# A fused two-block transformer layer on one core: where small side products of TensorE stand

## The reference

```
sh1, sc1, gt1, sh2, sc2, gt2 = split(silu(c) @ w_mod + b_mod, 6)       # w_mod: 1024 x 6144
csh1, csc1, ...              = split(silu(c_ctx) @ w_mod + b_mod, 6)
h  = rmsnorm(x, g_pre1)   * (1 + sc1)  + sh1
hc = rmsnorm(ctx, g_pre1) * (1 + csc1) + csh1      # ctx: 256 context tokens
q, k, v, f, g_a, g_f = split(h @ w_in);  kc, vc = split(hc @ w_in[:, k and v])
attn = banded_window_attention(rope(q), rope(k), v, kc, vc, sink)
y = (sigmoid(g_a) * (attn @ w_pa) + sigmoid(g_f) * (fourier_mix(f) @ w_pf)) @ w_out
x = x + gt1 * rmsnorm(y, g_post1)
h2 = rmsnorm(x, g_pre2) * (1 + sc2) + sh2
x = x + gt2 * rmsnorm(conv_ffn(h2), g_post2)
```

## Time and profile before

| | us |
|---|---|
| median of 3 runs | 1402.28 (1400.53 to 1405.31) |
| profiled execution: its time | 1401.24 |
| profiled execution: span | 1399.5 |
| TensorE busy | 1372.2 (98%) |
| DVE busy | 839.5 (60%) |
| ACT busy | 636.2 (45%) |

### The profile page before, as it was taken

How to read it: one execution, slowest core, us unless ns; L and a number is a source line. 1 busy time by engine, 2 the same in 40 slices (tenths; PEclk the granted TensorE clock), 3 DMA queues, 4 the chain that set the end, 5 groups by cost and what they waited for, 6 DMA issues and landing times.

```text
span 1399.5 us, 17278 instructions
## 1 busy us (share of the span) xinstructions
PE 1372.2 (98%) x6886; PEld 1116.6 (80%) x6886; DVE 839.5 (60%) x1272; ACT 636.2 (45%) x1032; POOL 26.9 (2%) x28
## 2 busy tenths in 40 slices
PE   8999999999999999999999999999999999999998
PEld 6777766788888888888987777887888888888887
DVE  6577887487766767665846444346466543444334
ACT  7435566554545444234534544444544333333234
POOL 3000000000003000000000000000000000000000
PEclk9999999999999999999999999999999999999999
DMA  6524220323222333663031111132214432222321
GB/s 242 203 83 135 76 76 31 121 106 124 102 89 92 98 98 124 237 211 121 31 129 61 47 61 61 60 121 90 91 44 136 142 115 90 94 102 91 105 91 61
DMA packets 46043, 146.71 MB, mean 105 GB/s; under 512 B 4971, under 2 KB 12139, under 8 KB 45580
## 3 DMA queue, kind: packets, MB, share of 16 engines
q1 hardware_dynamic: 45676, 145.08, 31.3%
q10 hardware_dynamic: 288, 0.52, 0.1%
HBM read 142.18 MB, written 3.41 MB: 104 GB/s over the span
## 4 chain that ended last, share of the span: by engine, by line
PE 88%; DVE 6%; ACT 3%; DMA 2%; issue 1%; SPq 0%; DVEq 0%; ACTq 0%
PE PS L351 26%; PE PS L352 25%; PE PS L353 25%; PE PS L1056 1%; PE PS L1047 1%; DVE wlo L317 1%; DVE mt L1713 1%; PE PS L566 1%; PE PS L1021 1%; ACT whi L301 1%; PE PS L1029 1%; PE PS L722 1%; PE PS L668 1%; PE PS L673 1%; PE PS L657 1%
## 5 line engine op out<-in xcount | busy, mean ns | idle before, releaser
L317 DVE TENSOR_TENSOR wlo<-raw,whi 128x1024 fp32r<-128x1024 f32 x205 | 251.8, 1233 | 340.7 <-ACT whi L301 340.5
L351 PE MATMUL PS<-Hhi,whi 128*128 128x512 f32 (+1 forms) x1136 | 435.9, 384 | 7.7 <-DVE Hlo L1719 5.8
L352 PE MATMUL PS<-Hlo,whi 128*128 128x512 f32 (+1 forms) x1136 | 425.3, 374 | 0.0
L353 PE MATMUL PS<-Hhi,wlo 128*128 128x512 f32 (+1 forms) x1136 | 425.0, 374 | 0.0
L301 ACT ACTIVATE whi<-raw 128x1024 fp32r<-128x1024 f32 x205 | 215.1, 1054 | 241.6 <-DMA raw<-in_w_down 114.3
L351 PEld LDWEIGHTS PS<-Hhi,whi 128*128 128x128 f32 x1136 | 216.3, 190 | 59.9 <-issue 15.1
L353 PEld LDWEIGHTS PS<-Hhi,wlo 128*128 128x128 f32 x1136 | 216.4, 190 | 38.1
L352 PEld LDWEIGHTS PS<-Hlo,whi 128*128 128x128 f32 x1136 | 216.6, 191 | 36.5 <-issue 1.2
L351 PE MATMUL PS<-Dhi,whi 128*128 128x512 f32 (+1 forms) x384 | 142.9, 372 | 0.0
L352 PE MATMUL PS<-Dlo,whi 128*128 128x512 f32 (+1 forms) x384 | 142.6, 371 | 0.0
L353 PE MATMUL PS<-Dhi,wlo 128*128 128x512 f32 (+1 forms) x384 | 142.6, 371 | 0.0
(11 more groups left out here) (410 smaller groups left out, 1833.2 us busy)
## 6 DMA issues: line engine op xcount, KB each, us to landing
raw<-in_w_up SPq DMA_DIRECT2D x88, 512.0 KB, 3.5
wm<-in_w_mod SPq DMA_DIRECT2D x48, 512.0 KB, 3.7
raw<-in_w_down SPq DMA_DIRECT2D x44, 512.0 KB, 3.5
raw<-in_w_g SPq DMA_DIRECT2D x16, 512.0 KB, 3.4
raw<-in_w_out SPq DMA_DIRECT2D x8, 512.0 KB, 3.5
raw<-in_w_o SPq DMA_DIRECT2D x8, 384.0 KB, 3.4
raw<-in_w_sk SPq DMA_DIRECT2D x4, 512.0 KB, 4.5
raw<-in_w_dq SPq DMA_DIRECT2D x4, 512.0 KB, 4.7
```

The lines of the kernel that those rows point to most:

```text
L317: e.tensor_tensor(wlo[i % NS], raw[i % NS], whi[i % NS].bitcast(f32), ALU.subtract).then_inc(q["w_lo"], 1)
L351: e.matmul(o, lhs[0], rhs[0], start=first, stop=False, skip_group_check=own)
L352: e.matmul(o, lhs[0], rhs[1], start=False, stop=False, skip_group_check=own)
L353: return e.matmul(o, lhs[1], rhs[0], start=False, stop=last, skip_group_check=own)
```

## The change

Five edits. (1) `acc_columns` multiplies with all 128 columns of ones instead of one; the extra columns land in unused parts of the bank. (2) Group 3's columns move from the attention loop to the end of the first output projection. (3) The context's key product moves into the end of `down(0, ...)`, ahead of the first `post_stat`, into the half of bank 6 that DVE's copy frees; DVE's copy moves behind its first sum; some statistics move from bank 6 to bank 4. (4) Groups 4 and 5 are done before the squares of half a, groups 6 to 9 behind them. (5) Loads and multiply-adds of the pieces 42 to 47 and the multiply-adds of 40 and 41 move into the second output projection, and the columns of groups 10 and 11 to its end.

```diff
+    SQ_BANK = {(0, "a"): 6, (0, "b"): 4, (1, "a"): 6, (1, "b"): 6}
-    T_COLUMNS = {9: 2, 14: 3}
+    T_COLUMNS = {9: 2}
@@ sync_program
         mod_load(e, 40)
         mod_load(e, 41)
-        load_to(e, ld, CH["w_up2"] + 6 + NS)
-        for n in range(42, 48):
-            load_to(e, ld, CH["w_up2"] + 6 + 2 * (n - 41) + NS)
-            mod_load(e, n)
+        for o, ns in enumerate(((42, 43), (44,), (45, 46), (47,))):
+            load_to(e, ld, CH["w_out2"] + o + NS)
+            for n in ns:
+                mod_load(e, n)
         load_to(e, ld, NCHUNK)
@@ acc_columns
-                    last = e.matmul(PS[:, bank, at + 2 * n + v:at + 2 * n + v + 1], mod_sum(g, v)[:, 128 * n:128 * n + 128],
-                                    ones[:, 0:1], start=True, stop=True)
+                    last = e.matmul(PS[:, bank, at + 2 * n + v:at + 2 * n + v + 128], mod_sum(g, v)[:, 128 * n:128 * n + 128],
+                                    ones, start=True, stop=True)
@@ tensor_program, first output projection
-                e.wait_ge(q["mod"], 4)
                 post_stat(7, 7, HALF["a"])
+        acc_columns(3, 5, 0)
         e.wait_ge(q["p_y"], 10)
...
+            if n == 5:
+                e.wait_ge(q["mod"], 4)
             chunk_product(e, CH["w_up"] + n, hx, n % 6)
@@ down
+        def context_product(i, bank, cols):
+            e.wait_ge(q["hc_lo"], 8)
+            e.wait_ge(q["w_lo"], i + 1)
+            for k in range(8):
+                last = products(e, PS[:, bank, cols], wtile(i, k), hcx(k), k == 0, k == 7)
+            last.then_inc(q["kvc_mm"], 1)
...
                     if h == "b" and i == 1:
                         e.wait_ge(q["p_yb"], layer + 1)
+                        if layer == 0:
+                            context_product(CH["w_k2"], 6, HALF["b"])
                         post_stat(PA[post] + 7, 6, HALF["a"])
@@ behind down(0)
-        e.wait_ge(q["p_y"], PY[1] + 15)
+        e.wait_ge(q["p_y"], PY[1] + 9)
+        acc_columns(4, 7, 0)
+        acc_columns(5, 7, 8)
         e.wait_ge(q["r_ln"], RS["p1a"])
         for c in range(8):
             squares_sum(0, "a", c, sq_a)
-            if c == 2 or c == 4:
-                acc_columns(3 + c // 2, 7, 8 * (c // 2 - 1))
-        e.wait_ge(q["hc_lo"], 8)
-        chunk_product(e, cK, hcx, 4, done=False, width=256).then_inc(q["kvc_mm"], 1)
+        for g in range(6, 10):
+            acc_columns(g, 7, 8 * (g - 4))
...
         e.wait_ge(q["r_ln"], RS["n0a"])
-        post_stat(PA[1] + 14, 6, HALF["b"])
+        e.wait_ge(q["p_y"], PY[1] + 15)
+        post_stat(PA[1] + 14, 4, HALF["b"])
         group_half_a(0, cs, sq_a)
...
         chunk_product(e, cV, hx, 4)
         rope(0, K2)
-        for g in range(6, 10):
-            acc_columns(g, 7, 8 * (g - 4))
         e.wait_ge(q["r_ln"], RS["n0b"])
         chunk_product(e, CH["w_q3"], hx, 6)
@@ behind the second output projection
+        acc_columns(10, 5, 0)
+        acc_columns(11, 5, 8)
         e.wait_ge(q["p_y"], PY[3])
         e.wait_ge(q["r_ln"], RS["n1a"])
         group_half_a(1, range(CH["w_up2"], CH["w_up2"] + 4), sq_b)
...
-            if n == 26:
-                e.wait_ge(q["r_ln"], RS["n1b"])
-                acc_columns(10, 6, 0)
-                acc_columns(11, 6, 8)
+            if n == 5:
+                e.wait_ge(q["mod"], 6)
@@ vector_program: down
+            def first_b():
+                o = DN_ORDER[0]
+                e.wait_ge(q["dn_o"], 15 * layer + 9)
+                ts(Y_A[:, o, HALF["b"]], PS[:, o, HALF["b"]], 1.0, 1.0, ALU.mult, ALU.mult, "p_yb")
             for i in range(1, 8):
                 post_sum(2 * layer + 1, i, i, i, HALF["a"])
+                if layer == 0 and i == 1:
+                    first_b()
@@ vector_program: second output projection and w_up2
         for o in range(6):
             split_to(CH["w_out2"] + o + AHEAD)
+            mod_part((4, 3, 3, 2, 2, 2)[o])
             if o:
                 post_sum(2, o, o, o, FULL)
...
         normed(1, "b", G2, lambda c: MOD[:, 24 + c, 0:1])
+        mod_adds(10, 12, 5)
+        e.wait_ge(q["mod"], 6)
+        tt(P2, MOD[:, 40:48, 0], vc("h_post2", n=8), ALU.mult, "gains")
...
-            if 6 <= n < 22:
-                mod_part(1)
-            if n == 27:
-                mod_adds(10, 12, 6)
```

More of the change, by code:

```diff
@@ L757, in first_heads @@
                 else:
-                    e.wait_ge(q["mod"], 4)
+                    e.wait_ge(q["mod"], 3)
             out_half(o, 0, i, O_BANK[o])
@@ L870, in tensor_program, with hcx @@
                 ctx_sum(7)
+        def hcx(k):
+            return HChi[:, k, :], HClo[:, k, :]
+        def context_product(i, bank, cols):
[4 more added lines that the diff above has]
+            last.then_inc(q["kvc_mm"], 1)
         def down(layer, i0, bank_free):
@@ L906, in squares_sum @@
             e.wait_ge(q["sq_a"], 16 * layer + nth(h) + c + 1)
-            e.matmul(PS[:, 6, HALF[h]], ones, sq[c][:, HALF[h]], start=c == 0, stop=c == 7).then_inc(q["sq_mm"], 1)
+            e.matmul(PS[:, SQ_BANK[layer, h], HALF[h]], ones, sq[c][:, HALF[h]], start=c == 0, stop=c == 7).then_inc(q["sq_mm"], 1)
         def group_half_a(layer, cs, sq):
@@ L943, in group_half_b @@
                 last.then_inc(q["w_done"], 1)
-        def hcx(k):
-            return HChi[:, k, :], HClo[:, k, :]
         cK, cV = CH["w_k2"], CH["w_v2"]
-        e.wait_ge(q["p_y"], PY[1] + 15)
+        e.wait_ge(q["p_y"], PY[1] + 9)
+        acc_columns(4, 7, 0)
+        acc_columns(5, 7, 8)
         e.wait_ge(q["r_ln"], RS["p1a"])
@@ L952, in tensor_program @@
             squares_sum(0, "a", c, sq_a)
-            if c == 2 or c == 4:
-                acc_columns(3 + c // 2, 7, 8 * (c // 2 - 1))
-        e.wait_ge(q["hc_lo"], 8)
-        chunk_product(e, cK, hcx, 4, done=False, width=256).then_inc(q["kvc_mm"], 1)
+        for g in range(6, 10):
+            acc_columns(g, 7, 8 * (g - 4))
         cs = [cK, CH["w_q2"], CH["w_q2"] + 1, CH["w_q2"] + 2]
         e.wait_ge(q["r_ln"], RS["n0a"])
-        post_stat(PA[1] + 14, 6, HALF["b"])
+        e.wait_ge(q["p_y"], PY[1] + 15)
+        post_stat(PA[1] + 14, 4, HALF["b"])
         group_half_a(0, cs, sq_a)
-        chunk_product(e, cV, hcx, 5, done=False, width=256).then_inc(q["kvc_mm"], 1)
+        context_product(cV, 5, HALF["a"])
         group_half_b(0, cs)
@@ L1174, in tensor_program @@
                 e.wait_ge(*up2_free(n - 6))
-            if n == 26:
-                e.wait_ge(q["r_ln"], RS["n1b"])
-                acc_columns(10, 6, 0)
-                acc_columns(11, 6, 8)
+            if n == 5:
+                e.wait_ge(q["mod"], 6)
             chunk_product(e, CH["w_up2"] + n, hx, n % 6)
         down(1, CH["w_down2"], [up2_free(42), up2_free(43), up2_free(38), up2_free(39), up2_free(40), up2_free(41),
-                                (q["mod"], 6), (q["r_ln"], RS["p2b"])])
+                                (q["r_ln"], RS["n1b"]), (q["r_ln"], RS["p2b"])])
         e.wait_ge(q["r_ln"], RS["p3a"])
@@ L1505, in norm_rstd @@
         def norm_rstd(layer, h):
-            rstd(G_r[:, HALF[h]], 6, HALF[h], q["sq_mm"], 16 * layer + nth(h) + 8, f"n{layer}{h}")
+            rstd(G_r[:, HALF[h]], SQ_BANK[layer, h], HALF[h], q["sq_mm"], 16 * layer + nth(h) + 8, f"n{layer}{h}")
         def normed(layer, h, c, shift):
@@ L1520, in scalar_program @@
             if c == 3:
-                post_rstd("p1b", 6, HALF["b"])
+                post_rstd("p1b", 4, HALF["b"])
         split_to(CH["w_q3"])
@@ L1530, in scalar_program @@
         e.wait_ge(q["kvc_mm"], 1)
-        act(KC, PS[:, 4, 0:256], ACT.Copy, "kvc_ev")
+        act(KC, PS[:, 6, 256:512], ACT.Copy, "kvc_ev")
         e.wait_ge(q["kvc_mm"], 2)
@@ L1962, in vector_program @@
             scaled_lo(h, 7)
+        mod_add(3, 5, 0)
         for c in range(1, 8):
@@ L2015, in down @@
             split_to(i0 + NF - 2 + AHEAD)
+            def first_b():
+                o = DN_ORDER[0]
+                e.wait_ge(q["dn_o"], 15 * layer + 9)
+                ts(Y_A[:, o, HALF["b"]], PS[:, o, HALF["b"]], 1.0, 1.0, ALU.mult, ALU.mult, "p_yb")
             for i in range(1, 8):
                 post_sum(2 * layer + 1, i, i, i, HALF["a"])
-            o = DN_ORDER[0]
-            e.wait_ge(q["dn_o"], 15 * layer + 9)
-            ts(Y_A[:, o, HALF["b"]], PS[:, o, HALF["b"]], 1.0, 1.0, ALU.mult, ALU.mult, "p_yb")
+                if layer == 0 and i == 1:
+                    first_b()
+            if layer:
+                first_b()
         def down_sums_b(layer, i0, i1):
@@ L2235, in vector_program @@
                 up2_second(n - 1)
-            if 6 <= n < 22:
-                mod_part(1)
-            if n == 27:
-                mod_adds(10, 12, 6)
-                e.wait_ge(q["mod"], 6)
-                tt(P2, MOD[:, 40:48, 0], vc("h_post2", n=8), ALU.mult, "gains")
         up2_second(2 * NF - 1)
```

## The result

The changed kernel takes 1408.2 us (median of 15 runs, 1404.35 to 1411.24) against 1402.74 us for the kernel before (15 runs, 1396.86 to 1405.43): ratio 1.0038, 95% interval 1.0028 to 1.0047. The forecast was 1407.3. One of the executions of the kernel before that ran beside e1 to e4 took 3838.14 us and is left out of what follows. The profiled execution took 1408.98 us with a span of 1407.2, 7.7 above that of before. Lines of functions behind the edits have new numbers: L351 to L353 are L353 to L355, L566 is L568, L710 is L712, L809 is L811, L907 is L923, L301 and L317 are L303 and L319, L284 is L286, L336 is L338, and ACT's and DVE's helpers moved by 12.

What follows compares the result with a forecast made beforehand. The prediction took TensorE, 88% of the span, to bound the kernel. Its terms, -0.1 + 0.2 + 0.2 - 7.4 + 14.2 + 1.3 - 1.7 - 1.7, gave +5.0 us, carried to the median 1407.3 us; range 1399 to 1413.

Steps and rivals of the forecast that it cites:

- Group 3: Attention loop to end of first output projection: moving its columns gains 0.1 us, as DVE's residual chain sets the later stretch.
- the reading of head_ln: Attention loop: transposes after group 3's columns wait for ACT's logarithm until 221.65, so removing the columns gains only 0.1 us.
- Wide columns: Groups 0, 1 and 2, which stay on the path: 128-column matmuls instead of one-column ones cost 0.2 us.
- Key product and groups 4 to 9: Down projection's end and next normalisation: key product fills TensorE's 2.58 us wait, DVE's moved copy delays statistics; cost 0.2 us.
- Just enough room: Before the next normalisation's Hlo: groups 6 to 9 (3.4 us) fit where the key product (2.9 us) stood.
- Columns at 711: At 711.83: 3.99 us of column matmuls and 3.4 us of low clock behind them vanish, gain 7.4 us.
- The load chain: Second output projection: each pass waits on landing, rounding, split, products and next load, delaying the statistics by 14.2 us.
- The other rival, landings of 3.5 us: Second output projection: passes chain, but each load lands in 3.5 us as alone; 1400.7 us, chance 0.17.
- Restart at low clock: After about 10 us of idle TensorE before the half-bank statistics, outputs 6 and 7 run partly at half speed: +1.3 us.
- Clock at 1018 and columns out of the up projection: Groups 10 and 11: leaving the up projection gains 1.7 us; busy TensorE keeping its clock at 1018 gains 1.7.
- Ring hides it: Second output projection: five weight slots keep chunks ahead, DVE never waits for a split; 1391.8 us, chance 0.10.
- Clock gain missing: The 3.4 us behind 711.83 are absent in most executions, or low clock appears elsewhere; 1410.7 us, chance 0.13.

Runs made afterwards that it cites:

- e1: Changed kernel with pieces 42 to 47, their products and the columns of groups 10 and 11 back in the up projection; 1395.34 us, ratio to before 0.9951.
- e4: Changed kernel with DVE's products put ahead of the weight split in each pass of the second output projection, SyncE's order untouched; 1390.74 us, ratio 0.9914.
- e9: e4 with group 3's columns back in the attention loop at t = 14, now 128 wide; 1390.67 us, ratio 0.9916.
- e12: Kernel before with only the 128-wide column matmuls, all in their old places; 1397.98 us, ratio 0.9963.
- e8: e4 with the key product back behind the columns of groups 6 to 9, in bank 4 as before; 1396.16 us, ratio 0.9956.
- e2: Kernel before with only the move of modulation loads and products, and of groups 10 and 11, into the second output projection; 1417.79 us, ratio 1.0113.
- e5: Changed kernel with SyncE loading pieces 42 and 43, then one piece behind each weight chunk; DVE's order untouched; 1410.31 us, ratio 1.0056.
- e10: e4 with only the columns of groups 10 and 11 back in the up projection (n = 26), 128 wide; 1395.14 us, ratio 0.9953.
- e7: e4 with the columns of groups 6 to 9 back behind the value product, and one-column matmuls in all groups; 1401.92 us, ratio 0.9988.
- e6: e4 with the columns of groups 6 to 9, 128 wide, back behind the value product and first rope; 1395.86 us, ratio 0.996.
- e11: e4 once more, unchanged, for comparison on the same chip; 1392.39 us, ratio 0.9929.
- e3: Changed kernel with both DVE's order (products ahead of split) and SyncE's (one piece behind each weight chunk after 42 and 43) altered; 1393.2 us, ratio 0.9934.

## Why the prediction was right, and which of its terms were off

The forecast was +5.0, the profiles differ by 7.7, the medians by 5.5. So the sum was 2.7 us short of the profiles that it was meant for, and that the median came within 0.9 us of the forecast is in part luck: before's profile lies 1.5 us under its median of 15 runs, the changed kernel's 0.8 above. The start gives -0.1 and the stages +0.07, +0.20, -6.79, +16.05, +1.52 and -3.22.

- Group 3, -0.1: right (S2 +0.07), and so is the reading of head_ln. What I missed is that this was the price of an unused chance: with wide columns the old place is worth 1.5 us (e9, e12), so moving the group away gave that up.
- Wide columns, +0.2: the sum holds only because the other edits take the columns out of dense streams. By itself edit (1) is worth -4.5 us in the median (e12; 1.5 in S2 and 3.5 in S4), nearly all of the 1.7 and 3.4 that the clock lost at 220 and 712. I had both rows ahead of me, that the low clock follows one-column matmuls, and put the gain down to the move alone.
- Key product and groups 4 to 9, +0.2: S3 grew by 0.20. "Just enough room" holds as well: with both in that room S4 is 2.9 us longer (e8), nearly all of it the key product.
- Columns at 711, -7.4: S4 gives -6.79. I counted 0.6 us twice: the 3.99 us of the columns already contained a part of the slow stretch (between the ropes 13.12 us became 6.35, that is 6.77).
- The load chain, +14.2: measured +16.05. The mechanism is shown by e2, e4 and e5. Of the sum, the fixed part was 23.2 us and is 22.6, the start 5.85 and 5.60; the four landings were taken as 20.6 and are 6.1 + 5.7 + 7.0 + 4.5 = 23.3. So this term, mis-sized by 1.85 us, is the largest error of the sum. The 4.4 us of the earlier trace rows was a bad value for the second pass: there one modulation load went ahead as well, and the landing took 5.7. The third, behind two modulation loads, took 7.0 where the earlier trace rows gave 5.9. What set them apart I didn't find out. The other rival, landings of 3.5 us, is out.
- Restart at low clock, +1.3: S6 +1.5. TensorE's idle time was not one wait of 10 us but two, 4.7 and 7.7; the first is for the split of w_out2+7, which I had put only some 2 us late. The granted clock is 0.51 and 0.53 over the stretches at the end of the waits and behind them. By the Trainium skill (TensorE: Matmul & The Clock Gate, What's actually happening) the throttled state is the default and activity releases it. The trace agrees, with these two figures.
- Clock at 1018 and columns out of the up projection, -3.4: S7 -3.2, and e10 takes it back with 3.3. The first half was right for a half-wrong reason: I wrote that a busy TensorE keeps its clock. e7 is as busy in the same place with one-column matmuls and loses it.
- Rivals: "Ring hides it" falls by the loads 10 to 11 us apart. "Clock gain missing" falls by e1, where the gain of some 6.5 stands in the median of 6 runs.

## What to carry to other kernels

When a transfer and the work that frees its buffer are moved into a loop, follow one pass around: if the freeing work stands behind work that needs the transfer queued after it, the loop runs at the sum of its latencies, here in spite of five weight slots; putting the freeing work first made 17 us here with no other change. Put small products where TensorE waits anyway, and make them full width there: the cover is worth their time (3.55 us between the ropes), and the width keeps the clock for what follows (1.6 to 3.2 us there).

## What the runs showed of the hardware

- Away from the kernel's start and end, the time lost to low clock is a multiple of 1.7 us at each place in all 14 profiles (1.7, 3.4, 5.1 or 8.5). A busy TensorE isn't safe from it: one-column float32 matmuls bring it though the engine shows no gap, not each time (at 168 in two of three narrow profiles, at 220 in one of two, at 712 in three of three, at 1166 in none of one), while no wide ones at these places had it right behind them. At 292, ahead of the statistics, the one narrow profile has it too (e7, 0.66 from 295 to 300) and the nine wide ones don't, with a wait of 0.65 us there in e7 and 0.54 in the others. Idle waits of 1.9 us (t = 14) bring it in nine of the ten profiles without columns there, the one of 2.9 us for Hlo behind the second output projection in every profile that has it (before, e1, e10, e12), one of 2.3 us ahead of the statistics at 294 in all four that have it (before, e2, e9, e12). But waits of 2.5 to 2.6 us at 661 bring it in none of three (before, e2, e12), and one of 2.9 there does (e8). So the length of a wait alone doesn't tell.
- Two equal programs differ by their start. The first column matmuls start at 67.5 to 67.6 in four of the profiles (before, after, e4, e6) and at 69.5 to 71.1 in the other ten, e4 (67.48) and e11 (70.35) being the same program. Part of it is the clock in the first microseconds: in the changed kernel the matmuls of 512 columns start 0.43 us apart up to 10 us and 0.23 apart from 11 on, in e11 they still start 0.43 apart at 16. Half of these 6 us is 3, and the columns are 2.9 apart. The granted clock of the profile reads 1.00 there in both, so in this stretch the pace of the matmuls has to be read instead. What sets the start beyond that, in e7 and e8 above all, no run shows. A pair of profiles is compared by stages, or 3 us of chance are read as an effect: the profiles of e3 and e4, 2.7 us apart, are equal in every stage within 0.3 us. That the start also makes the 2.5 us between their medians is likely, but not shown.
